# DeltaNet layer of a two-block transformer: the eight gate blocks cut into one piece a round over rounds 60 to 107, the conditioning steps placed in rounds 5 to 113

## The reference, cut to what matters

```python
def project(h):
    p = h @ w_in
    qkv = silu(_centred_dwconv(p[..., :n_qkv], conv_w))      # q, k l2-normed
    z = p[..., n_qkv:n_qkv + hv]                             # the gate: no convolution
    ...
for d in range(2):                                           # two directions, context then latent
    s0 = 0
    def step(s, inp):                                        # one chunk, all heads
        v_new = u_n - w_n @ s
        o_n = qd_n @ s + qk_n @ v_new
        s = s * exp(gl_n) + kd_n.T @ v_new
out: o = rmsnorm(o_forward + o_backward) * silu(z); y = o @ w_out
conditioning: (silu(c) @ ada_w[i] + ada_b[i]) split in 6, for layers i = 0, 1
```

## Time and profile before

| what | us |
|---|---|
| median of 3 runs (range) | 4184.85 (4183.09 to 4189.86) |
| the profiled execution | 4193.0, its span 4191.2 |
| PE busy over the span | 3883.7 (93%) |
| DVE, ACT, POOL busy | 2150.9, 1665.2, 617.2 |
| the unit sequence, rounds 0 to 137 | 197.5 to 858.3 |
| rounds 0 to 59, 60 to 99 | 302.0, 204.9 |
| rounds 100 to 113, 114 to 137 | 62.7, 91.2 |

### The profile page before, as it was taken

One profiled execution on the slowest core, in us unless ns is written; L12 is line 12 of the kernel. 1 busy time (PEld: TensorE's weight loads), 2 busy tenths in 40 slices (PEclk: granted clock), 3 DMA queues, 4 the chain that ended last, 5 costly groups with the idle time before them and its releaser, 6 DMA issues.

```text
span 4191.2 us, 67651 instructions
## 1 busy us (share of the span) xinstructions
PE 3883.7 (93%) x28266; PEld 3189.0 (76%) x28266; DVE 2150.9 (51%) x3078; ACT 1665.2 (40%) x2708; POOL 617.2 (15%) x676
## 2 busy tenths in 40 slices
PE   6999999788999988987899899999999998899999
PEld 4877777677888866756788675778888878778887
DVE  3667754753222453377323654555665428655564
ACT  4445454322112242263323346554334335544333
POOL 0045554422000001003000000000210003000120
PEclk8999999798999999999999899999999999999999
DMA  4254553221121121103222320231323230312332
GB/s 162 89 170 147 159 167 125 70 89 61 61 70 51 61 87 51 50 1 112 81 94 93 71 81 11 73 101 62 101 94 106 90 111 3 130 65 81 101 101 81
DMA packets 235991, 367.67 MB, mean 88 GB/s; under 512 B 9811, under 2 KB 142630, under 8 KB 235302
## 3 DMA queue, kind: packets, MB, share of 16 engines
q1 hardware_dynamic: 217200, 300.49, 21.9%
q0 software_dynamic: 17936, 62.70, 4.8%
q10 hardware_dynamic: 550, 0.17, 0.0%
HBM read 344.36 MB, written 18.96 MB: 87 GB/s over the span
## 4 chain that ended last, share of the span: by engine, by line
PE 76%; DVE 13%; ACT 7%; issue 1%; DMA 1%; ACTq 0%; POOL 0%; DVEq 0%; SPq 0%; POOLq 0%
PE psum L259 21%; PE psum L260 20%; PE psum L261 20%; PE psum L256 13%; DVE arena L289 3%; ACT arena L389 3%; PE psum L265 2%; DVE arena L299 2%; DVE rw L289 2%; DVE rx L383 2%; ACT arena L393 1%; DVE arena L303 1%; ACT rw L393 1%; ACT rx L393 1%; DVE arena L315 1%
## 5 line engine op out<-in xcount | busy, mean ns | idle before, releaser
L259 PE MATMUL psum<-rx,rw 128*128 128x512 f32 (+2 forms) x2864 | 1056.9, 369 | 55.2 <-DVE rx L383 29.3
L260 PE MATMUL psum<-rx,rw 128*128 128x512 f32 (+2 forms) x2864 | 1030.8, 360 | 0.0
L261 PE MATMUL psum<-rx,rw 128*128 128x512 f32 (+2 forms) x2864 | 1029.4, 359 | 0.0
L289 DVE TENSOR_TENSOR rw<-arena,rw 128x2048 fp32r<-128x2048 f32 (+3 forms) x266 | 546.5, 2054 | 811.7 <-ACT rw L393 802.1
L256 PE MATMUL psum<-arena 32*32 32x32 f32 (+11 forms) x12982 | 767.9, 248 | 120.3 <-ACT arena L393 48.0
L256 PEld LDWEIGHTS psum<-arena 32*32 32x32 f32 (+5 forms) x12982 | 586.2, 134 | 260.2 <-issue 83.7
L393 ACT ACTIVATE rw<-arena 128x2048 fp32r<-128x2048 f32 (+3 forms) x266 | 453.6, 1705 | 754.5 <-PE psum L261 739.6
L259 PE MATMUL psum<-rw,rx 128*128 128x512 f32 (+1 forms) x1720 | 682.0, 396 | 31.1 <-DVE rx L383 13.8
L259 PEld LDWEIGHTS psum<-rx,rw 128*128 128x128 f32 (+1 forms) x2864 | 550.5, 192 | 191.9 <-DVE rx L383 42.7
L260 PE MATMUL psum<-rw,rx 128*128 128x512 f32 (+1 forms) x1720 | 673.4, 392 | 0.0
L261 PE MATMUL psum<-rw,rx 128*128 128x512 f32 (+1 forms) x1720 | 673.1, 391 | 0.0
(11 more groups left out here) (73 smaller groups left out, 2204.4 us busy)
## 6 DMA issues: line engine op xcount, KB each, us to landing
arena<-in_ffn_w_up SPq DMA_DIRECT2D x66, 1024.0 KB, 5.1
arena<-in_ada_w SPq DMA_DIRECT2D x48, 1024.0 KB, 6.1
arena<-in_ffn_w_down SPq DMA_DIRECT2D x40, 1024.0 KB, 4.9
arena<-in_ffn_w_gate SPq DMA_DIRECT2D x22, 1024.0 KB, 5.1
arena<-in_dn_w_in SPq DMA_DIRECT2D x16, 1024.0 KB, 5.8
arena<-in_xa_w_kv SPq DMA_DIRECT2D x16, 1024.0 KB, 5.0
arena<-in_hgrn_w_in SPq DMA_DIRECT2D x16, 1024.0 KB, 5.4
arena<-in_da_w_in SPq DMA_DIRECT2D x12, 1024.0 KB, 5.1
```

The costliest lines, as they stand in the source:

```text
L259: self.e.matmul(out, l[0], r[0], start=start, stop=False)
L260: self.e.matmul(out, l[0], r[1], start=False, stop=False)
L261: return self.e.matmul(out, l[1], r[0], start=False, stop=stop)
L289: return self.e.tensor_tensor(out, a, b, op)
```

## The change

Three schedules move; no product is added or left out.

- **Gate blocks.** Each takes six rounds, one piece a round (`Z_STEPS`): four pieces of 6 wide matmuls, two of 12 narrow ones. The eight blocks fill rounds 60 to 107; before, they took rounds 60 to 98. Each bank is emptied on its own, by ACT 4 and 6 rounds after the block's start, and the store follows at 7. The weights are taken at 62, 74 and 86 instead of 60, 70 and 80.
- **Conditioning.** The 60 steps skip the first of every four groups of five rounds below 60 (rounds 0 to 4, 20 to 24, 40 to 44) and go on to round 113. Nine steps leave those groups and stand in rounds 100 to 113.
- **Tails.** The first six start up to three rounds later: 104, 106, 110, 112, 114, 117 for 101, 104, 107, 110, 113, 116. The others stay. Since the gates now use another buffer and end later, DVE's output sum waits for the first gate's store in chunk 3 and for the last one's in chunk 1.

```diff
+    if r > FIRST_Z:
+        return K.mem(WK + 2316, 768)
...
-        a.wait_ge(*K.at("z_st", r - 1) if STREAM[r - 1][2] == Z_ else K.at("dn_tok", r - 1))
+        if r == FIRST_Z:
+            a.wait_ge(*K.at("dn_tok", r - 1))
+        else:
+            a.wait_ge(*K.at("tok_st", FIRST_Z - 1))
+            if r > FIRST_Z + 1:
+                a.wait_ge(*K.at("z_st", r - 1))
...
     if hg and c == 3:
+        v.wait_ge(*K.at("z_st", FIRST_Z))
+    if hg and c == 1:
         v.wait_ge(*K.at("z_st", STREAM.index((1, 3, Z_))))
-    if hg and c == 1:
-        v.wait_ge(*K.at("tok_st", STREAM.index((1, 3, V_))))
...
+def z_rounds(rnd, offset):
+    r = FIRST_Z + (rnd - offset - Z_FROM) // 6
+    return r if (rnd - offset - Z_FROM) % 6 == 0 and FIRST_Z <= r < len(STREAM) else None
+FIRST_Z, Z_FROM = 24, 60
+Z_STEPS = [(0, (0, 1)), (0, (2, 3)), (0, (4, 5)), (0, (6, 7)), (1, (0, 1, 2, 3)), (1, (4, 5, 6, 7))]
-SIDE_ROUNDS = [r for r in range(100) if r % 5 in (0, 2, 3)]
+SIDE_ROUNDS = [r for r in range(115) if r % 5 in (0, 2, 3) and (r >= 60 or r // 5 % 4)]
...
-    r = DENSE + rnd // GAP
+    if rnd < Z_FROM:
+        r, steps = DENSE + rnd // GAP, STEPS.get(rnd % GAP, ())
+    else:
+        r, step = divmod(rnd - Z_FROM, 6)
+        r, steps = r + FIRST_Z, Z_STEPS[step:step + 1]
...
+    for s in range(2):
+        r = z_rounds(rnd, 4 + 2 * s)
+        if r is not None:
             act_part_raw(a, K, r, s)
...
-    r = part_rounds(rnd, 5)
-    if r is not None and STREAM[r][2] == Z_:
+    r = z_rounds(rnd, 7)
+    if r is not None:
```

More of the change, by code:

```diff
@@ L2196, in pe_between @@
         p.wait_ge(*K.at("lo", m))
-        for s, ks in STEPS.get(rnd % GAP, ()):
+        for s, ks in steps:
             pe_part_steps(p, K, r, m, s, ks, PART_BANKS[s:s + 1])
@@ L2218, in act_between @@
         ms.append(a.skip())
-    if rnd < 90 and rnd % 10 in (2, 4, 7):
-        for q in {2: (0,), 4: (1,), 7: (2, 3)}[rnd % 10]:
-            a.split_quarter(ms[-1], q)
+    for q in {2: (0,), 4: (1,), 7: (2, 3)}.get(rnd - max([t for t in TILE_ROUNDS if t <= rnd]), ()):
+        a.split_quarter(ms[-1], q)
     if rnd in (119, 122):
@@ L2231, in act_between @@
     r = part_rounds(rnd, 8)
-    if r is not None and STREAM[r][2] != Z_:
+    if r is not None:
         act_part_silu(a, K, r)
-    if rnd < 60:
-        r = part_rounds(rnd, 3)
+    for s in range(2):
+        r = part_rounds(rnd, 3 + s)
         if r is not None:
-            act_part_raw(a, K, r, 0)
-    r = part_rounds(rnd, 4)
-    if r is not None:
-        for s in range(0 if STREAM[r][2] == Z_ else 1, 2):
+            act_part_raw(a, K, r, s)
+        r = z_rounds(rnd, 4 + 2 * s)
+        if r is not None:
             act_part_raw(a, K, r, s)
@@ L2262, in dve_between @@
         ms.append(v.skip())
-    if rnd < 90 and rnd % 10 in (3, 5, 8):
-        for q in {3: (0,), 5: (1,), 8: (2, 3)}[rnd % 10]:
-            v.split_quarter(ms[-1], q)
+    for q in {3: (0,), 5: (1,), 8: (2, 3)}.get(rnd - max([t for t in TILE_ROUNDS if t <= rnd]), ()):
+        v.split_quarter(ms[-1], q)
     if rnd in (120, 123):
```

6 lines of the change are left out of this document (3 added, 3 removed).

## The result

The changed kernel takes 4181.94 us (median of 22 runs, 4176.62 to 4187.82), the kernel before, run beside it, 4190.23. The ratio is 0.9982, 95% interval 0.9976 to 0.9988: 8.3 us, 0.18%, where 22.1 us were forecast, and 1.9 us above the range. What failed is the size of the forecast gain. The profiled execution took 4181.2 us.

The account below looks back on a forecast made before the run. PE, busy 3883.7 us, was taken to set the pace, except in rounds 100 to 113, where the chain through other engines did. Terms -20.0 - 6.5 + 4.4 - 1.5 + 1.5 = -22.1 us gave 4162.7 us; range 4149 to 4180.

Parts of the forecast that it names:

- ACT's own queue: Rounds 60 to 99: single Silus and table loads between Exp and copies are covered by PE's work; charged nothing.
- the pieces: Rounds 60 to 99: eight gate pieces leave, 11.5 us gained; a piece covering DVE's turn waits gains 1.5 us.
- The wait for the bank and its cold clock: Rounds 60 to 99: PE's waits for Silus emptying the bank go, 7.2 us, and slow matmuls after one, 2.3 us.
- wrong if PE waits for ACT's copies in rounds 67, 77 and 97: Sign against the forecast: PE waiting for ACT's copies in these rounds would show it wrong; no size given.
- The loads of `ada_w`: Rounds 60 to 99: loads for the second conditioning half come late in two groups; 2.5 us charged, bounds 0 and 14.
- Rounds 0 to 59 (-6.5): Nine conditioning steps leave three groups of rounds, gaining 6.5 us; bounds 0 and 9.
- a collision moves: Rival: a small shift makes or ends a long set of DVE copies, 3 to 6 us either way; no separate chance.
- mostly new waits: Rival: shorter rounds turn most of the gain into waits for loads, DVE and ACT; 4170 to 4180 us, chance 0.20.
- ACT becomes the bound: Rival: Silu pieces delay copies PE needs; all 16 exposed cost 30 us, giving 4193 us; chance 0.09.
- Rounds 100 to 113 (+4.4, -1.5): Rounds 100 to 107 gain work, +4.4 us; rounds 108 to 113 cover four steps and run warmer, -1.5 us.
- Rounds 114 to 137 (+1.5): Tails starting closer together add DVE arithmetic where DVE answers last; 1.5 us longer.

Follow-up runs that it names:

- both_after: Changed kernel with 32x32 transposes for VectorE's four diagonal copies and the four clamps in a unit's first round, except the very first unit; 4150.55 us.
- clamp_after: Changed kernel with VectorE's four clamps of a unit moved from the end of its second round to the end of its first; 4166.45 us.
- nosilu_after: Changed kernel with the gate's Silu replaced by a plain copy of the same size, which also removes its table loads; 4173.55 us.
- kq_after: Changed kernel with GpSimd's k and q loads of rounds 61, 66, 71 and 76 issued two rounds later; 4180.82 us.
- turn_after: Changed kernel with VectorE's four diagonal block copies written as 32x32 transposes giving the same numbers; 4163.3 us.
- both_z: Changed kernel with conditioning steps back on their old rounds, plus transposes for the four copies and clamps a round earlier except the first unit's; 4159.47 us.
- both_before: Kernel before the change with transposes for the four copies and clamps a round earlier, except the very first unit's; 4173.36 us.

## Why the prediction was wrong

Two steps failed. One is the term for ACT's own queue in rounds 60 to 99, "I cost them at nothing"; that stage came 7.7 us short of its forecast. The other is the collision of VectorE's copies with GpSimd, which stood in the range and at nothing in the sum; rounds 0 to 59 came 8.4 us short by it.

**Rounds 60 to 99, the pieces (11.5 and 1.5 us).** Right: 12.4 us between the two kernels without Silus.

**The wait for the bank and its cold clock (9.5 us).** The rows went as said: no wait of L259, and rounds 85 to 89 took 23.2 us for 29.2. The gain did not stay. The groups of rounds 65 to 69 and 75 to 79 took 25.8 and 29.3 us, and 22.4 and 23.4 in both_after: 9.3 of the 10.3 us between the two kernels' rounds 60 to 99. By round, 2.0 us are in round 65, behind held copies; 1.3 and 1.4 in rounds 67 and 77, whose ends hold the waits for ACT's copies; and 4.4 in rounds 78 and 79, at the slow clock.

The step "I cost them at nothing" let PE's work cover load, Silu and two copies, 2.6 us, as if the Exp ahead of them came in time. It came 2.3 us late in round 76, behind a clamp that GpSimd held. The argument for cover summed ACT's own operations and never asked when the first of them could start; PE's work covered 2.6 us but not 4.9. This was not a thing that the change brought: in the trace of the kernel before the same Exp was 2.4 us late, for the same reason, and one clamp each of rounds 66, 71 and 76 took 2.5 us. clamp_after (clamps moved, Silus kept) and nosilu_after (Silus gone, clamps kept) each take the waits away, so it takes both. The check "wrong if PE waits for ACT's copies in rounds 67, 77 and 97" had the right mechanism with rounds 68 and 78 in its place.

How much such a wait costs was partly luck: behind 2.47 us of it the changed kernel's round 78 took 8.9 us at a clock of 0.50, behind 2.12 in kq_after 6.4 at 0.73, and behind 2.65 in turn_after 4.8 at 1.00.

**The loads of `ada_w` (2.5 us charged).** 0.2 us in rounds 60 to 99; too cautious. 2.3 us showed in round 112, where none was charged.

**Rounds 0 to 59 (-6.5).** Rounds 20 to 24 and 40 to 44 fell by 2.9 and 3.3 us, as counted. Rounds 25 to 29 and 45 to 49 gave 5.6 and 5.3 back, to held copies. With transposes in place of the copies and the clamps moved, both_after takes 4.8 us less than both_z there, near the forecast. The pair's -11.0 is more than the change: 7.3 us of it lie in rounds 0 to 14, where both_before waited longer for loads of `ada_w` (4.3 us, 1.7 in both_z) although both_z has the same lists there. What makes that difference stays open.

**The rival "a collision moves".** This is what happened to the copies: the changed kernel has three more held sets of them, in rounds 25, 45 and 64. It is not what happened to the clamps, which were held as long before. The sum took the rival as 3 to 6 us either way, from one pair of rows, and put it into the range. What a collision costs is not the 2.4 us by which the copies are longer: it is PE's wait and then, where the clock falls, the rounds at 1.2 GHz. The long copies of round 39 in the earlier trace rows had that price in the kernel before already: rounds 35 to 44 took 59.9 us there and 50.3 in both_before.

By whole kernels, the transpose alone took 18.6 us from the changed kernel, the clamps' move alone 15.5, and the two together 31.4; together they took 17 from the kernel before. The difference of 14 us is the size of what was missed, each of the two good to some 5 us by its interval. It is no clean price of collisions: the clamps' move also freed copies, and the 17 would be larger by whatever of the 7.3 us of rounds 0 to 14 is not the schedule's.

**That both_before and both_after differ by 22.8 us, next to the forecast of 22.1,** is in part luck. Rounds 60 to 99 bear the forecast out (-21.9 for -20.0); of the rest, 4.5 us too much in rounds 0 to 59 and 6.7 too little from round 114 on nearly cancel.

**The rival "mostly new waits" (4170 to 4180)** came nearest in number and had the wrong mechanisms: neither the loads nor an average lateness of DVE and ACT, but five single stalls (rounds 25, 45, 65, 68, 78). Its range does not follow from its own figures either: 9 to 17 us gained, less 6.5, is 4174 to 4182.

**The rival "ACT becomes the bound"** had the mechanism of rounds 68, 78 and 107, a piece that delays what PE needs next, and the wrong size: it wanted all 16 pieces exposed.

**Rounds 100 to 113 (+4.4, -1.5).** +4.9 and -2.5; right, and by the named means: PE busy at 0.96 and 0.93. The wait that was left in the sum is the load and Silu of round 106.

**Rounds 114 to 137 (+1.5).** +1.1, but by luck: between both_before and both_after these rounds cost 8.2 us, of which two tails account for half.

**The direction** and the size of the fills in rounds 60 to 107 were right.

## What to carry to other kernels

Before moving work in a schedule of strict lists, list the operations whose longest case is several times their median, see what runs beside them when they are long, and price a collision with PE's wait and, as a range, the cold stretch behind it (here 2.5 us of wait, and between nothing and 4 us more in the round behind it). If they can be made immune (another form of the same operation) or be moved a round ahead of whoever waits, do that first: the two edits were worth 17 us to the old schedule and 31 to the new one, where the change alone gained 8. When costing an operation as covered, start the sum at the time at which its predecessor really ends in the worst row, not at its place in the list; here that row was in the trace of the kernel before.

## What the runs showed of the hardware

- VectorE's 32x128 copies and 128x128 clamps take 0.31 and 0.29 us at the median and up to 1.45 and 2.64 beside GpSimd. The 38 in the changed kernel's unit sequence that took over 0.4 us ended 0.02 to 0.21 us after a product or a DMA issue of GpSimd. Transposes are not held: 216 of 216 in both_after within 0.299 to 0.315 us, those of the same 32x128 blocks among them. The Trainium skill's page "SBUF — State Buffer", section "Who interferes with whom", says that a copy or a tensor_scalar on VectorE can enter a mode that takes the port pair which it shares with GpSimd, and that the one that gets the pair second is blocked for the other's whole instruction. The trace agrees as far as the products go.
- VectorE is also held while GpSimd issues DMAs: six clamps of the changed kernel met an issue and no product, took 0.41 to 0.59 us, and ended 0.03 to 0.06 us after the issue. The clamp of round 76 began at 580.79, during an issue that ended at 581.10, and was held through the next issue and then through a product that began 1.07 us after the clamp; here the product, which came second, got ahead.
- A wait of PE of 2.47 us was followed by a granted clock of 0.50 for 9.3 us (587.5 to 596.8) and a round of 8.9 us; one of 2.65 us in turn_after, at the same place in the lists, by a clock of 1.00 and a round of 4.8.
